# Two-layer mixer and expert kernel: earlier picks for the context tokens, attention heads in pairs, and the latents' query products and key scores split by tile

## The chip, the cores and the metric

One core of one Trainium2 chip runs one launch. The metric is the device time of that launch in microseconds (us); lower is better. The figure for a kernel is the median of its runs.

## What is computed

The reference is one step of a network with two layers over 128 context tokens and 512 latent tokens, 1024 features each, all in 32-bit floats. Per layer and per group of tokens:

```python
h = rmsnorm(x, P['norm_mix_g']) * (1.0 + sc_m) + sh_m
proj = h @ P['w_in']
# attention (8 query heads, 2 key/value heads, 64 wide), hyena (long convolution by FFT), chunked gating
mixed = jnp.concatenate([attn, hy, sg], axis=-1) @ P['w_out']
x = x + g_m * mixed
h = rmsnorm(x, P['norm_ffn_g']) * (1.0 + sc_f) + sh_f
x = x + g_f * peer(h, P['peer_wq'], P['peer_keys'], P['peer_u'], P['peer_v'])
```

and in `peer`, for each token and each of 8 heads:

```python
q = (x @ wq).reshape(T, PEER_HEADS, 2, PEER_HALF)
s = jnp.einsum('thpd,hpnd->thpn', q, keys)          # 2 x 128 scores
s_top, i_top = lax.top_k(s, 16)                     # 16 of each 128
cand = s_top[..., 0, :, None] + s_top[..., 1, None, :]
sc, pos = lax.top_k(cand, 16)                       # 16 of 256
gate = softmax(sc)
a = gelu(einsum('td,ted->te', xt, u_tab[idx]))      # 16 rows of 1024 per token and head
out = einsum('te,ted->td', gate * a, v_tab[idx])    # 16 more
```

The latents' attention has 128 cached and 512 own keys; the context's has its own 128. The convolution's filter is made from a small network of sines (jobs f1, f2, f3) and a transform (job hf), and does not depend on the tokens.

## The kernel before, in words

**Tiles and groups.** The 640 tokens are five tiles of 128: four of latents (index L_ = 0) and one of context (C_ = 1). The work is two kinds of job. A mixer job is one product with what follows it (qk, vt, hy, su, df, cv, attention, wo, the second norm, wq, ka and kb). An expert step is one unit, which is one head of one tile: 16 experts for each of 128 tokens. There are four groups of units, `GROUPS` = context of layer 0 (8 units), latents of layer 0 (32), context of layer 1 (8), latents of layer 1 (32), 80 units in all.

**One expert step** (`step_jobs`, L175). Step u has 16 pieces. Each has a `dot` of unit u on VectorE (L1415: the gathered row times the token's features, summed) and an `add` of unit u-1. For context units the add is one VectorE operation (L1429); for latent units it is two products on TensorE by a diagonal (L885), whose diagonal ScalarE makes from an identity (L1113). Between the pieces VectorE picks the experts of unit u+1: `stage` (ScalarE copies 256 scores, L1094), then six parts of `pick` (L1373 and on) with 27 linked steps: the 16 best of each 128 scores, the 16 best of the 256 sums, and the index by one-hot rows (L1395 to L1398, twice over 256 elements). Last in a step come `weigh` and `gexp`.

**The gathers.** GpSimd issues 32 indirect transfers per unit (`fetch`, L610), one u row and one v row in turn, each 128 rows of 4 KB. Rows land in a ring of 4 places per table, so a transfer is issued when a dot or an add has freed its place, and GpSimd waits in order.

**The weights.** SyncE streams blocks of 1 MB through a ring of 4 slots (`STREAM`, L298). A block is issued when the last product of the block four places ahead is done. The 0.5 MB of expert keys is the last block of each mixer. Before layer 1's blocks, `small_loads` waits for the latents' last kb.

**The order.** `ORDER` (L225) is one list that every engine walks in order, taking its part of each job. `weave` puts expert jobs between mixer jobs in proportion to the costs in `ROOM`. In sequence:

- the context's mixer of layer 0 alone, then the pick of unit 0 (`start_jobs`);
- the latents' mixer of layer 0, woven with the 9 steps of the first context group (units 0 to 7 of the trace);
- the context's mixer of layer 1, woven with steps 0 to 16 of the first latent group (units 8 to 24);
- steps 17 to 32 of that group alone (units 25 to 39 and the last adds), then the pick of unit 40;
- the latents' mixer of layer 1, woven with the second context group (units 40 to 47);
- the second latent group alone (units 48 to 79), and the output.

In the latents' mixers all of wq (8 jobs of 8 products, 512 columns, L700) comes first, then ka and kb (L865: scores of 4 heads, ka from rows 0 to 63, kb from rows 64 to 127). The first latent unit is picked after the scores of tile 0, and its first dot waits for `ht` (L872), the transpose of the tile's features.

**Attention of the latents.** 32 units, one head and one tile each: scores over 640 keys with 64 rows of the array (L813, L814), the maximum on VectorE (L1334), the exponential on ScalarE (L1075), a reciprocal and a diagonal on VectorE (L1339, L1343), five transposes that also scale (L823), a copy on ScalarE (L1082), and five products with the values that fill 64 of the output's rows (L835). Scores of unit n+3 wait for the copy of unit n.

**TensorE in 32-bit.** Every product shows as two records in the trace.

## Time and profile before

| | us |
|---|---|
| median of 3 runs | 4240.7 |
| lowest and highest | 4236.87, 4241.16 |
| the profiled execution | 4239.37 |
| its span, first to last instruction | 4237.5 |

The profiled execution lies 1.3 us below the median, and the span leaves 1.9 us of it outside. Busy time is the time in which an engine runs an instruction. In windows, each engine has its busy time and, in brackets, its number of instructions; PEclk is the share of 2.4 GHz that TensorE's clock was granted, and the last number is what the DMA engines moved in GB/s. In lines of the timeline, the number in square brackets is how long the engine stood idle before, and what ended that.

### The profile page before, as it was taken

The numbers are of one execution on the slowest core, as the hardware profiler recorded it, in microseconds if no ns is written. First come the engines' busy times: TensorE is split into PE (matmuls) and PEld (weight loads), VectorE is DVE, ScalarE is ACT, GpSimd is POOL, SyncE is SP. The second block draws the span as 40 slices with busy tenths as digits, with TensorE's granted clock in tenths as the row PEclk, the third lists the DMA queues.
The fourth block names the chain that finished last, engine by engine and source line by source line (L and its number), as shares of the span: only waits on it lengthen the run. The fifth ranks groups of instructions, "written<-read, shape, count | busy, mean of one in ns | idle before, by whom it ended". The sixth has DMA issues, their size and how long they took to land.

```text
span 4237.5 us, 33926 instructions
## 1 busy us (share of the span) xinstructions
PE 3274.7 (77%) x9680; PEld 1513.7 (36%) x9680; DVE 2951.7 (70%) x6826; ACT 1065.3 (25%) x2256; POOL 2563.5 (60%) x2564
## 2 busy tenths in 40 slices
PE   6797896577778787777776978975777777777777
PEld 4653653233333333222222536542222222222223
DVE  2388998545667666677764889897676767677673
ACT  4322322122222222222223323221222222222222
POOL 0054666345656666777773545566777777777774
PEclk8898998689999999999998988987999999999999
DMA  7587788899989999999995877788999999999998
GB/s 281 215 314 276 262 297 287 330 378 369 381 332 384 379 407 386 408 409 401 409 407 191 318 277 244 275 303 336 409 407 395 407 409 400 409 406 401 401 409 313
DMA packets 394007, 1485.64 MB, mean 351 GB/s; under 512 B 44124, under 2 KB 46878, under 8 KB 377952
## 3 DMA queue, kind: packets, MB, share of 16 engines
q0 software_dynamic: 368640, 1342.34, 82.5%
q1 hardware_dynamic: 25184, 141.13, 8.6%
q8 instruction: 81, 1.33, 0.1%
q14 instruction: 102, 0.84, 0.1%
HBM read 1480.42 MB, written 2.88 MB: 350 GB/s over the span
## 4 chain that ended last, share of the span: by engine, by line
DMA 25%; DVE 21%; PE 19%; POOL 18%; issue 13%; ACT 4%; SPq 0%; DVEq 0%; ACTq 0%; POOLq 0%
POOL rows_ring L610 18%; DMA rows_ring<-in_peer_u,idx 13%; DMA rows_ring<-in_peer_v,idx 11%; PE psum L885 8%; DVE rows_ring L1415 7%; DVE mix L1429 4%; PE psum L700 4%; PE psum L687 1%; PE psum L823 1%; DVE small L1334 1%; PE psum L656 1%; DMA ring<-in_ada 1%; DVE pos L1362 1%; DVE pos L1359 1%; DVE cand L1360 1%
## 5 line engine op out<-in xcount | busy, mean ns | idle before, releaser
L885 PE MATMUL psum<-rows_ring,diag 128*128 128x512 f32 x4096 | 2042.7, 627 | 674.9 <-DMA rows_ring<-in_peer_v,idx 544.5
L610 POOL DMA_INDIRECT rows_ring<-in_peer_u,idx x1280 | 1298.0, 1014 | 1015.5 <-DVE rows_ring L1415 475.3
L1415 DVE SCALAR_TENSOR_TENSOR rows_ring<-rows_ring,psum 128x1024 f32<-128x1024 f32 x1024 | 1240.7, 1220 | 678.9 <-DMA rows_ring<-in_peer_u,idx 639.7
L610 POOL DMA_INDIRECT rows_ring<-in_peer_v,idx x1280 | 1265.2, 988 | 634.2 <-issue 306.6
L885 PEld LDWEIGHTS psum<-rows_ring,diag 128*128 128x128 f32 x4096 | 717.3, 193 | 1937.6 <-DMA rows_ring<-in_peer_v,idx 1231.7
L1113 ACT ACTIVATE diag<-ident,wts 128x128 f32<-128x128 f32 x1024 | 382.3, 397 | 1333.3 <-PE psum L885 1332.6
L700 PE MATMUL psum<-area,ring 128*128 128x128 f32 (+1 forms) x1344 | 386.7, 447 | 15.6 <-ACT area L975 14.9
L1429 DVE SCALAR_TENSOR_TENSOR mix<-rows_ring,wts,mix 128x1024 f32<-128x1024 f32 x254 | 326.4, 1285 | 15.5 <-DMA rows_ring<-in_peer_v,idx 13.9
L1415 DVE SCALAR_TENSOR_TENSOR rows_ring<-rows_ring,area 128x1024 f32<-128x1024 f32 x256 | 311.9, 1222 | 13.5 <-DMA rows_ring<-in_peer_u,idx 12.0
L700 PEld LDWEIGHTS psum<-area,ring 128*128 128x128 f32 x1344 | 216.3, 200 | 195.0 <-issue 191.7
L700 PE MATMUL psum<-mix,ring 128*128 128x128 f32 (+1 forms) x512 | 143.0, 441 | 2.9 <-DVE mix L1354 2.1
L1105 ACT ACTIVATE acts<-dots 128x16 f32<-128x16 f32 x80 | 17.3, 216 | 498.4 <-DVE rows_ring L1415 498.3
L823 PE MATMUL psum<-sg_junk,area 128*128 128x128 f32 x672 | 109.5, 314 | 37.0 <-DVE sg_junk L1343 37.0
L823 PEld LDWEIGHTS psum<-sg_junk,area 128*128 128x128 f32 x672 | 93.5, 214 | 53.8 <-DVE sg_junk L1343 43.5
L1101 ACT ACT_TABLE_LOAD x75 | 96.2, 1283 | 41.0 <-DVE wts L1440 41.0
L700 PEld LDWEIGHTS psum<-mix,ring 128*128 128x128 f32 x512 | 80.8, 198 | 67.3 <-issue 63.6
L835 PE MATMUL psum<-area,v_tok 128*64 128x128 f32 x672 | 102.4, 304 | 0.0
L1075 ACT ACTIVATE area<-psum,small 128x640 f32<-128x640 f32 (+1 forms) x80 | 56.9, 711 | 176.0 <-DVE small L1334 175.9
L1105 ACT ACT_TABLE_LOAD x78 | 100.1, 1283 | 1.4
L813 PE MATMUL psum<-area 64*128 64x512 f32 x128 | 81.6, 720 | 13.3 <-ACT area L1082 6.7
L1082 ACT COPY area<-psum 128x640 f32<-128x640 f32 (+1 forms) x80 | 48.5, 606 | 161.3 <-PE psum L823 161.3
L835 PEld LDWEIGHTS psum<-area,v_tok 128*64 128x64 f32 x672 | 81.4, 152 | 15.7 <-issue 9.3
(176 smaller groups left out, 2497.3 us busy)
## 6 DMA issues: line engine op xcount, KB each, us to landing
ring<-in_ada SPq DMA_DIRECT2D x48, 1024.0 KB, 8.2
ring<-in_win SPq DMA_DIRECT2D x32, 1024.0 KB, 8.1
rows_ring<-in_peer_u,idx POOLq DMA_INDIRECT x1280, 7.2
rows_ring<-in_peer_v,idx POOLq DMA_INDIRECT x1280, 7.1
ring<-in_wout SPq DMA_DIRECT2D x16, 1024.0 KB, 8.0
ring<-in_wq SPq DMA_DIRECT2D x16, 1024.0 KB, 7.8
ring<-in_dft SPq DMA_DIRECT2D x12, 1024.0 KB, 7.8
xT<-in_xT_in SPq DMA_DIRECT2D x1, 2048.0 KB, 13.1
```

Source lines behind the costliest of these rows:

```text
L610: pool.indirect_dma_start(row(table, k), None, (peer_u, peer_v)[table], bass.IndirectOffsetOnAxis(ap=idx[u % IDX_PLACES][:, k:k + 1], axis ...
L700: m = pe.matmul(g[:, 0:WIDTH[st]], w[:, k * P:(k + 1) * P], src(k), start=(k == 0), stop=(k == KC - 1))
L813: pe.matmul(g[:, 0:512], q, kT[st][rows, 0:512], start=True, stop=True)
L823: m = pe.matmul(att_bank(st, n)[:, b * P:(b + 1) * P], probs[st][:, n % 2, b * P:(b + 1) * P], softmax_diag[:, n % 2, :], start=True, stop ...
L835: m = pe.matmul(out_bank(st, c)[rows, t * P:(t + 1) * P], v_tok[:, b, rows], probsT[st][:, n % 2, i * P:(i + 1) * P], start=(i == 0), stop ...
L885: m = pe.matmul(acc[:, b, :], diag[:, k % 4, :], row(1, k)[:, b * 512:(b + 1) * 512], start=(u % PEER_HEADS == 0 and k == 0), stop=last)
L1075: act.activation(probs[st][:, n % 2, :], att_bank(st, n)[:, 0:KEYS[st]], ACT.Exp, bias=negmax[:, n % 2:n % 2 + 1], accum_out=rowsum[:, n % ...
L1101: act.activation(gate_e[:], best[:], ACT.Exp, bias=gate_s[:, 1:2], accum_out=gate_s[:, 0:1]).then_inc(s["gexp_ready"], 1)
L1105: act.activation(acts[:], dots[:], ACT.Gelu_apprx_tanh).then_inc(s["gelu_ready"], 1)
L1113: act.activation(diag[:, k % 4, :], ident[:], ACT.Copy, scale=wts[:, k:k + 1]).then_inc(s["diag_ready"], 1)
L1415: dve.scalar_tensor_tensor(out=row(0, k), in0=row(0, k), scalar=1.0, in1=h, op0=ALU.mult, op1=ALU.mult, accum_out=dots[:, k:k + 1]).then_i ...
L1429: m = dve.scalar_tensor_tensor(out=out_tok[C_], in0=x, scalar=wts[:, k:k + 1], in1=out_tok[C_], op0=ALU.mult, op1=ALU.add)
```

## The change

- **Picks.** The scores are read where they lie, without the copy on ScalarE. The pick has 8 parts with 24 links, and the two one-hot halves are one operation over 512 elements. The 8 units of the second context group are picked in steps 21 to 28 of the first latent group, each behind that step's own pick, into index and gate places of their own (`idx_c`, `gate_c`). No `start_jobs` stands ahead of that group.
- **Filter.** Layer 1's filter jobs (f1, f2, f3, hf; 2 MB of transform blocks) move from the latents' mixer to steps 26 to 32 of the first latent group.
- **Attention.** The latents' heads go in pairs. Two heads' scores alternate between rows 0 to 63 and 64 to 127 of the array and end in different PSUM banks, and their value products alternate between output rows 0 to 63 and 64 to 127. The softmax diagonal moves from VectorE to ScalarE. The next scores wait for the copy of the pair two ahead of them.
- **Query products and scores.** wq of the latents covers the first tile's 128 columns, followed by that tile's scores and the pick. The other 384 columns (8 jobs wr) and the 12 other score jobs are woven with steps 0 to 3 of the latent group. The latents' keys go to the place of `sq` and not through the ring. ka and kb are issued alternately, head by head. The context's layer 1 mixer is woven with steps 4 to 20 instead of 0 to 16.

```diff
+    if st == L_:
+        n = ATT_UNITS[L_] // 2
+        jobs = [("fence", l, st, 0), ("pas", l, st, 0), ("pas", l, st, 1)]
+        for m in range(n):
+            jobs += [("pat", l, st, m)] + ([("pav", l, st, m - 1)] if m else [])
+            jobs += [("pas", l, st, m + 2)] if m + 2 < n else []
...
...
+def filter_jobs(l):
...
...
-        jobs += js("f3:0 f3:1 f3:2 f3:3 hf:0 hf:1 hf:2 hf:3")
+        jobs = js("rms:0 app:0") if l else js("f3:0 f3:1 f3:2 f3:3 hf:0 hf:1 hf:2 hf:3")
         jobs += js("qk:0 vt:0 hs:0 vt:1 vt:2 rot:0 vt:3 hy:0 ck:0 hy:1 hy:2 hy:3 hy:4 hy:5 su:0 ut:0 su:1 ut:1 "
                   "qk:1 sp:0 hs:1 qk:2 rot:1 hs:2 qk:3 rot:2 hs:3 qk:4 rot:3 hs:4 sp:1 df:0 rot:4 df:1 df:2 df:3 cv:0 cv:1")
...
+        if st == L_ and i == 1:
+            return jobs
...
+def late_jobs(l):
...
+    jobs = [("wr", l, L_, j) for j in range(KC)]
+    for i in range(2, 2 * LAT_TILES):
+        jobs += [("ka", l, L_, i), ("kb", l, L_, i)]
+    return jobs
...
+PICK_AT = (0, 1, 3, 4, 6, 7, 9, 10)
...
+PICKED_AHEAD = (2,)
+AHEAD_FROM = 21
...
+    own = u + 1 < n and grp not in PICKED_AHEAD
...
-        jobs += [("pick", grp, u + 1, p // 2)] if u + 1 < n and p % 2 and p // 2 < PICK_PARTS else []
+        if own and ahead and p < PICK_PARTS:
+            jobs += pick_jobs(grp, u + 1, [p])
+        elif own and not ahead and p in PICK_AT:
+            jobs += pick_jobs(grp, u + 1, [PICK_AT.index(p)])
+        if ahead and p >= PICK_PARTS:
+            jobs += pick_jobs(*ahead, [p - PICK_PARTS])
...
+    jobs += [("gexp", grp, u + 1, 0)] if own else []
+    jobs += [("gexp", *ahead, 0)] if ahead else []
...
+        v = u - AHEAD_FROM
+        early = grp + 1 in PICKED_AHEAD and 0 <= v < UNITS[grp + 1]
+        out += step_jobs(grp, u, (grp + 1, v) if early else None)
...
-    _a = 0
+    _a = LATE_STEPS
+    ORDER += weave(late_jobs(_l), expert_jobs(_g, range(_a)))
     if _l + 1 < DEPTH:
-        _a = PEER_HEADS * 2 + 1
-        ORDER += weave(mixer_jobs(_l + 1, C_), expert_jobs(_g, range(_a)))
-    ORDER += expert_jobs(_g, range(_a, UNITS[_g] + 1))
-    if _l + 1 < DEPTH:
-        ORDER += start_jobs(_g + 1)
...
+        ORDER += weave(mixer_jobs(_l + 1, C_), expert_jobs(_g, range(LATE_STEPS, _a)))
+        ORDER += expert_jobs(_g, range(_a, FILTER_FROM))
+        _a = FILTER_FROM
+        ORDER += weave(filter_jobs(_l + 1), expert_jobs(_g, range(_a, UNITS[_g] + 1)))
+    else:
+        ORDER += expert_jobs(_g, range(_a, UNITS[_g] + 1))
...
+                if (kind, st, i) == ("wq", L_, 3):
...
+                    sp.dma_start(sq_cols[:, :], keysT[l].rearrange("p a b -> p (a b)")).then_inc(s["keys_loaded"], 16)
...
+            def pair_scores(l, st, m):
...
+                for n, a, b in ((2 * m, 512, 640), (2 * m + 1, 128, 640), (2 * m, 0, 512), (2 * m + 1, 0, 128)):
+                    c, rows, t = unit_of(st, n)
+                    if (a, b) == (0, 128):
+                        pe.wait_ge(s["pair_first"], done("pas", l, st, m))
+                    ins = pe.matmul(att_bank(st, n)[:, a:b], qT[st][rows, c, t * P:(t + 1) * P], kT[st][rows, a:b], start=True, stop=True)
...
+                blocks = [TILES, 0, 1, 2, 3]
+                for i, b in enumerate(blocks):
+                    for n in (2 * m, 2 * m + 1):
+                        _, rows, _ = unit_of(st, n)
+                        ins = pe.matmul(out_bank(st, c)[rows, t * P:(t + 1) * P], v_tok[:, b, rows], probsT[st][:, n % 2, i * P:(i + 1) * P],
+                                        start=(i == 0), stop=(i == len(blocks) - 1))
+                ins.then_inc(s["pair_out"], 1)
...
+                project(st, half_of(blk("wq", l, st, j // 2), j % 2), g, lambda k: hT[st][:, k, 0:P], "h_ready",
+                        KC * NUMBER["app", l, st, 1], width=P).then_inc(s["wq_mm"], 1)
+            def wr(l, st, j, g):
+                project(st, half_of(blk("wq", l, st, j // 2), j % 2), g, lambda k: hT[st][:, k, P:LAT], width=LAT - P
+                        ).then_inc(s["wr_mm"], 1)
...
+                    for half, rows in ((0, slice(0, 64)), (1, slice(64, P))):
+                        m = pe.matmul(out[half][:, h * P:(h + 1) * P], mix[rows, h0 + h, a:a + P], keys[rows, h0 + h, :],
+                                      start=True, stop=True)
+                        if h == 3:
+                            m.then_inc(s[("ka_mm", "kb_mm")[half]], 1)
...
+            def pair_diag(l, st, m):
+                for n in (2 * m, 2 * m + 1):
+                    act.wait_ge(s["pair_rinv"], 2 * NUMBER["pat", l, st, m] + n % 2 + 1)
+                    act.activation(softmax_diag[:, n % 2, :], ident[:], ACT.Copy, scale=rinv[:, n % 2:n % 2 + 1]
+                                   ).then_inc(s["pair_diag"], 1)
...
                 step(dve.max(vals[:, 8:16], src))
                 step(dve.max_index(idxs[:, 8:16], vals[:, 8:16], src))
-            def pick(grp, u, to, part):
...
+                if part < 4:
+                    half = part // 2
+                    vals, idxs = topv[:, half, :], topi[:, half, :]
+                    src = scores[st][:, (2 * u + half) * N_KEYS:(2 * u + half + 1) * N_KEYS]
+                    if part % 2 == 0:
+                        top8(vals, idxs, src, step)
+                        step(dve.match_replace(src, vals[:, 0:8], src, -3.0e38))
...
+                    step(dve.tensor_tensor(pair, iota16.unsqueeze(1).unsqueeze(1).broadcast_to(two),
+                                           posf.unsqueeze(3).broadcast_to(two), ALU.is_equal))
...
-                    half, oh = part - 4, grid(onehot[:, :], TOPK)
-                    step(dve.tensor_tensor(oh, iota16.unsqueeze(1).broadcast_to(square),
-                                           posf[:, half, :].unsqueeze(2).broadcast_to(square), ALU.is_equal))
-                    step(dve.tensor_tensor(oh, oh, topf[:, half, :].unsqueeze(1).broadcast_to(square), ALU.mult))
-                    step(dve.tensor_reduce(picked[:, half, :], oh, AX.X, ALU.add))
...
+                    step(dve.tensor_tensor(pair, pair, topf.unsqueeze(2).broadcast_to(two), ALU.mult))
+                    step(dve.tensor_reduce(picked, pair, AX.X, ALU.add))
...
+                    dve.tensor_scalar(idx_of(grp, u), idxf[:], float(l * N_EXPERTS), None, ALU.add).then_inc(s["idx_ready"], 1)
```

## Rows read from the trace of the kernel before

**Rows 1.** The page: GB/s in 40 slices of the span.

```profile
GB/s 281 215 314 276 262 297 287 330 378 369 381 332 384 379 407 386 408 409 401 409 407 191 318 277 244 275 303 336 409 407 395 407 409 400 409 406 401 401 409 313
```

**Rows 2.** Windows by stage: length, busy us (x instructions), PEclk, DMA share, GB/s.

```profile
211.70:774.40 562.70, 460.16 (x1761) 276.96 (x1765) 484.73 (x918) 145.35 (x248) 318.82 (x257) 0.88 0.80 285
774.40:1627.80 853.40, 644.39 (x1980) 298.14 (x1979) 527.94 (x1362) 206.13 (x500) 502.03 (x532) 0.92 0.97 376
1627.80:2247.30 619.50, 476.40 (x980) 165.59 (x980) 431.71 (x1058) 141.44 (x327) 450.00 (x475) 1.00 1.02 404
...
2284.20:2870.50 586.30, 479.75 (x1769) 286.27 (x1769) 511.46 (x986) 167.83 (x279) 309.25 (x260) 0.86 0.74 266
```

**Rows 3.** Windows inside the second layer's latent mixer.

```profile
2304.00:2358.00 54.00, 32.49 (x91) 19.98 (x92) 44.62 (x101) 14.95 (x21) 17.65 (x15) 0.68 0.43 139
2358.00:2531.00 173.00, 150.74 (x478) 82.56 (x476) 153.50 (x286) 52.12 (x81) 90.31 (x77) 0.94 0.82 303
2531.00:2698.00 167.00, 143.29 (x768) 108.45 (x768) 152.08 (x312) 57.44 (x109) 93.00 (x76) 0.85 0.73 249
2698.00:2754.00 56.00, 55.51 (x130) 24.66 (x131) 47.95 (x88) 3.25 (x7) 32.39 (x29) 1.00 0.85 318
...
2769.00:2827.00 58.00, 57.25 (x128) 25.03 (x128) 54.92 (x71) 14.24 (x22) 41.20 (x37) 0.96 0.92 347
```

**Rows 4.** Windows inside the first layer's latent mixer.

```profile
648.00:714.00 66.00, 57.89 (x129) 25.18 (x129) 51.73 (x67) 13.86 (x22) 46.17 (x35) 0.91 0.84 287
714.00:774.40 60.40, 27.64 (x164) 22.02 (x168) 37.77 (x73) 7.36 (x14) 23.31 (x17) 0.57 0.71 244
```

**Rows 5.** Timeline, second layer's start: start, us, operation, idle before.

```profile
2284.16 0.28 DVE L1358 MAX8 topv<-unit_s 128x8 f32<-128x128 f32 x1
...
2294.67 0.17 DVE L1402 TENSOR_SCALAR idx<-idxf 128x16 uint32<-128x16 f32 x1
...
2308.82 1.22 DVE L1415 SCALAR_TENSOR_TENSOR rows_ring<-rows_ring,area 128x1024 f32<-128x1024 f32 x1
```

**Rows 6.** Timeline, VectorE: the first dot of the first latent group.

```profile
774.45 1.22 DVE L1415 SCALAR_TENSOR_TENSOR rows_ring<-rows_ring,psum 128x1024 f32<-128x1024 f32 x1 [13.69 <-PE psum L872]
```

**Rows 7.** Lines of VectorE, 2308 to 2871: busy us, mean ns, idle.

```profile
L1343 DVE TENSOR_SCALAR sg_junk<-ident,small 128x128 f32<-128x128 f32 x32 | 9.9, 311 | 1.1
L1397 DVE TENSOR_TENSOR onehot<-onehot,topf 128x256 f32<-128x256 f32 x16 | 6.8, 425 | 0.5
...
L1326 DVE COPY area<-psum 128x512 f32<-128x512 f32 x8 | 5.5, 684 | 0.9 <-PE psum L865 0.9
...
L1202 DVE SCALAR_TENSOR_TENSOR area<-area 64x512 f32<-64x512 f32 x6 | 4.1, 683 | 0.2
```

**Rows 8.** Lines of TensorE, the same stretch.

```profile
L687 PE MATMUL psum<-area,ring 128*128 128x256 f32 x128 | 32.7, 421 | 5.3 <-issue 5.3
L865 PE MATMUL psum<-ring,mix 64*128 64x128 f32 x128 | 18.9, 370 | 16.1 <-DVE area L1326 8.8 <-ACT area L1068 6.5 <-ACT mix L1064 0.7
```

**Rows 9.** Timeline, TensorE: the query products of the second layer.

```profile
2769.07 57.25 PE L700 MATMUL psum<-area,ring 128*128 128x512 f32 x128 [7.32 <-ACT area L975]
```

**Rows 10.** Timeline, TensorE: adds of latent experts alone.

```profile
2247.32 8.85 PE L885 MATMUL psum<-rows_ring,diag 128*128 128x512 f32 x20 [0.54 <-DMA rows_ring<-in_peer_v,idx]
```

**Rows 11.** Timeline, TensorE: two column halves taken in turn.

```profile
326.31 1.09 PE L767 MATMUL psum<-sgwT,sg_v 128*64 128x128 f32 x16
```

**Rows 12.** Timeline, TensorE: one attention unit.

```profile
487.19 1.31 PE L835 MATMUL psum<-area,v_tok 128*64 128x128 f32 x10
488.43 1.12 PE L813 MATMUL psum<-area 64*128 64x512 f32 x2
489.39 0.38 PE L814 MATMUL psum<-area 64*128 64x128 f32 x2
```

**Rows 13.** The page: a diagonal made on ScalarE, and the landing of a row.

```profile
L1113 ACT ACTIVATE diag<-ident,wts 128x128 f32<-128x128 f32 x1024 | 382.3, 397 | 1333.3 <-PE psum L885 1332.6
...
rows_ring<-in_peer_v,idx POOLq DMA_INDIRECT x1280, 7.1
```

More of the change, by code:

```diff
@@ L111, in phase @@
     return 2 * l + (st == L_)
+FILTER_FROM = 26
+LATE_STEPS = 4
+def filter_jobs(l):
+    return [("f1", l, L_, 0), ("f2", l, L_, 0)] + [(k, l, L_, t) for k in ("f3", "hf") for t in range(LAT_TILES)]
 def mixer_jobs(l, st):
@@ L241 @@
     _count[_job[0]] = NUMBER[_job] + 1
+    if _job[0] == "pick":
+        PICK.setdefault(_job[1:3], len(PICK))
+LAST_GEXP, _last = {}, {}
+for _job in ORDER:
+    if _job[0] == "pick" and _job[3] == 4:
+        LAST_GEXP[_job[1:3]] = _last.get(GROUPS[_job[1]][1])
+    elif _job[0] == "gexp":
+        _last[GROUPS[_job[1]][1]] = _job
 def done(*job):
```

296 lines of the change are left out of this document (191 added, 105 removed).

## The prediction

> **What bounds the kernel now.** I read the page's 40 slices first (106 us each), then windows by stage. The page shows long stretches at 400 to 410 GB/s, and two valleys: below 331 up to slice 8, and at 191 to 336 in slices 22 to 28 [rows 1]. No row anywhere exceeds about 410, so where the gathers run at that rate, only fewer bytes or a removed stop help. The stage windows give the boundaries [rows 2]:
>
> - 211.7 to 774.4, layer 0's latent mixer with 8 context units: 562.7 us at 285 GB/s, VectorE busy 484.7, TensorE 460.2.
> - 774.4 to 1627.8, 17 latent units with a context mixer: 853.4 us at 376 GB/s.
> - 1627.8 to 2247.3, 15 latent units alone: 619.5 us at 404 GB/s, so 41.3 us a unit. VectorE is busy 431.7, or 28.8 us a unit.
> - 2284.2 to 2870.5, layer 1's latent mixer: 586.3 us at 266 GB/s, VectorE 511.5, TensorE 479.8.
>
> Inside the mixers the bound moves [rows 3]. Attention (2531 to 2698) has VectorE busy 152.1 of 167. Projections and convolution (2358 to 2531) have both engines at 150 to 154 of 173. The stage of w_out and that of the query products are TensorE's: 55.5 of 56 and 57.3 of 58. So work taken from VectorE shortens the two mixers, and the split query products shorten a stage that TensorE holds.
>
> **The change, part by part.** The sum is against the profiled 4239.4 us, 1.3 below the median.
>
> *The pick.* One pick alone runs from 2284.16 to 2294.84, 10.7 us [rows 5]. Six operations over 256 elements at 0.43 become three over 512, for which the nearest row is a copy at 0.68 [rows 7]: 0.5 us less, so 10.2. No row shows a 512-wide one-hot; at twice 0.43 it saves nothing, and I take 0.5. Beside the latents' experts it lies in slack; in the first mixer 8 picks give 4 us.
>
> *Layer 1's latent mixer.* Off VectorE go the pick of unit 40 (10.7) and 7 more (about 10 of busy time each, 70), 32 diagonals of 0.31 (9.9), 6 of 8 key copies at 0.68 (4.1), and the filter: two chains of three operations at 0.68 and four shorter ones (estimated at 4.2 each), and four times one of 0.68 and two of 0.43 (6.2), 14.5 in all [rows 5, 7]. That is 109, leaving 402 of 511. Of VectorE's 75 us of idle time, the 9 around the filter chain, 6 of the 8 under w_out and 2 of the 3 beside wq go [rows 3], and I add 6 where picks filled gaps, as ahead of the first norm: its chain still ran 14.0 us past the pick's end [rows 5]. So 402 + 64 = 466: a gain of 120. Against it stand in-order waits and the DMA: w_out to wq have 884 of the mixer's 2528 `ROOM` points, so 35% of the 134 MB of rows (256 transfers of 0.52), plus 8 MB of weights, 55 MB or 135 us at 409 GB/s, where VectorE alone would allow about 130. I take 105, and keep 120 as one end and 75 as the other (all removed work but a third given back as waits).
>
> *Layer 0's latent mixer.* Its picks and filter stay. Off VectorE go 9.9, 4.1 and 4. The wq stage has VectorE idle for 14.3 of 66 us with TensorE at 57.9, and the last stage ends in 13.7 us of idle VectorE before the first dot [rows 4, 6], where the transposes stand in TensorE's queue behind products whose weights were requested only after the last kb. Of the 14.3 I count 11 as gone, with TensorE's share cut to a quarter, and of the 13.7 all, as unit 8 starts behind tile 0's scores; w_out, as above, gives 6. The total is 18 + 11 + 14 + 6 = 49, of which I take 40; ends 20 and 50. The wait for those weights does not vanish: it falls into step 4 of the latent group, where TensorE's adds queue behind it. I charge 5 there.
>
> *Attention pairs.* An existing line shows column pairs: 16 records with the halves alternating take 1.09 us, 10 one-sided ones of the same size 1.31 [rows 11, 12], so the value products about halve, 20 us of TensorE a layer. No row shows two row groups at once; between serial and halved, scores of 1.34 us a unit [rows 12] save 0 to 21. As VectorE holds the stage, I credit neither on the path. ScalarE gains 32 diagonals at 0.40 [rows 13], 13 us on an engine busy 57.4 of 167 [rows 3]: hidden, but each diagonal is now one more hop between engines; with dots and adds between the hops I price that at nothing; if they run dry, 0.3 us on each of 32 units is 10 a layer. The Trainium skill (TensorEngine Tiling, Overview) gives up to 2x for a contraction of 64 rows, which no row here shows for row groups. Read as the gain of the stage, that page gives the rival of paired products below, 4069 us. The same page (PSUM Bottleneck) says that tiling does not speed up the emptying of PSUM, and by that, as by VectorE's 152.1 of 167 us there [rows 3], the time stays as summed.
>
> *The late jobs, twice.* Eight wr jobs are 3/4 of the 57.3 us of wq [rows 9], 43 us, and the key jobs 3/4 of 18.9 [rows 8], 14. TensorE is busy 31.8 of 41.3 us in a unit alone [rows 2], so four steps have 38 spare, and 57 do not quite fit. The nearest row is the context mixer's stage: 104 us of TensorE above the adds' share, 42 MB of weights (103 us), 853.4 us against 17 x 41.3 + 103 = 805. So 48 lost for 104 us of mixer. That price gives 26; the low end is 0, since much of TensorE's busy time is its waiting tail. I take 15 per layer, 30 in all. ScalarE's and VectorE's copies (0.4 to 0.7 each) hide in slack.
>
> *Steps 21 to 32.* Two picks raise VectorE from 28.8 to about 39 of 41.3 us: nearly full, so 6 over eight steps. Filter work of 14.5 falls mostly on steps 26 to 28, with 7 spare: 7. The transform has half of the 32.7 us of its line [rows 8], four jobs of 4 us on TensorE, with the short ones 26 us: 7 for its stops. The 2 MB of blocks cost 5 at 409 GB/s, in the stage that is DMA-bound. Sum 25, ends 10 and 50.
>
> *The start.* About 1, for a lighter pick and no staged copy.
>
> Sum: -1 - 40 + 15 + 5 + 25 - 105 + 15 = -86, so 4153 us.
>
> **The rivals.**
>
> *Freed time turns into waiting.* VectorE's work is gone, but TensorE's order, its clock and the hops hold the mixers. For it: projections have TensorE at 150.7 of 173 [rows 3], and the granted clock is 0.85 in attention [rows 3] and 0.57 in layer 0's key stage [rows 4], where TensorE is least busy; fewer products may leave it more often at the lower of its two levels. Against: TensorE also loses about 120 us in layer 1 (43 + 14 + 26 + 20 and the scores' part). The mixers would give 20 and 60 instead of 40 and 105: 4218.
>
> *Slower: long TensorE jobs empty the gather rings.* Place: the 16 wr jobs in the first four steps of each latent group. Each is 5.4 us between adds, GpSimd stops on the next v row, and a new row takes 7.1 us to land [rows 13]. If each job costs its length and half a landing, 8.9, the 16 cost 143 instead of the 30 that all late jobs have in the sum: 4153 + 113 = 4266. It decides against the change from about 8 us a job. Against: 8 rows in flight are 10 us of DMA, and an add's pair of products takes 1.8 us where it doesn't wait (20 records, four to an add, in 8.85 [rows 10]) while the DMA brings a u and a v row in 2.6 (41.3/16), so TensorE catches up; weights of similar length ran beside experts at 376 GB/s.
>
> *VectorE overflows in steps 21 to 28.* If two picks and the dots no longer hide in the DMA's pace and a step takes 46 us, eight steps cost 38 where 6 stand: 4185.
>
> *Everything fits.* Late jobs and filter cost 15 together, and the mixers give 120 and 49: 4239 - 1 - 169 + 15 + 5 = about 4090.
>
> *Paired products on the path.* If TensorE held attention, halved scores and value products (32 x 1.34 and 32 x 1.31 us a layer [rows 12], 42 of 85) would come on top: 4153 - 84 = 4069. Against it: VectorE's load there.
>
> *The change does little*, because attention stays serial or the picks wait for something: covered by the first.
>
> **How the numbers follow.** Chances: forecast 0.53, freed time waiting 0.17, slower 0.08, overflow 0.08, all fits 0.11, pairs on the path 0.03. The forecast's own range by its bounds is 4110 to 4205. The range to hold 8 in 10 takes most of the good and the first bad rival: 4090 to 4222. A change of 0.2%, 8.5 us, is what a measurement of this kernel can tell from none: faster 0.88, the same 0.04, slower 0.08.
>
> **What would show it.** Right: the first dot of unit 8 near 734, that of unit 40 at most 20 us after the last latent add, unit 48 some 465 to 490 us after the end of group two's last adds; steps 21 to 28 at 42 to 44 us; no pick lines between units 40 and 47; steps 0 to 3 of each latent group at 43 to 48 us, with GpSimd's waits on TensorE grown there. Wrong: idle VectorE of over 100 us in either mixer, steps of over 50 us, or GB/s under 350 in a latent group's first four steps.

## The result, and the profile after

The changed kernel takes 4276.0 us (median of 4 runs, 4274.3 to 4282.3) against 4238.8 of the kernel before, run beside it: a ratio of 1.0093, 95% interval 1.0076 to 1.0111. It is slower by 0.9%; the forecast was 4153, and its range ended at 4222.

The profiled execution took 4274.3 us, with a span of 4272.5. The page's GB/s in 40 slices, after:

```profile
GB/s 283 228 323 272 266 317 261 310 328 366 389 350 387 376 377 372 390 384 382 334 368 364 262 322 308 335 230 315 344 409 398 409 408 400 409 405 402 406 409 311
```

The valley of layer 1's mixer is shallower (262, 322, 308, 335 in slices 23 to 26, where there were 318, 277, 244, 275 [rows 1]). But the level ahead of it has gone: slices 17 to 21, five times 401 or more before, now stand at 390 to 334. And slices 8 and 9, the first steps of the latent group, fell from 330 and 378 to 310 and 328.

Windows by stage, after (length, busy us and instructions of each engine, granted clock, DMA share, GB/s):

```profile
207.00:742.30 535.30, 367.79 (x1677) 235.03 (x1677) 471.76 (x859) 144.01 (x269) 306.60 (x257) 0.84 0.80 287
742.30:934.90 192.60, 130.73 (x381) 61.48 (x382) 118.00 (x283) 31.87 (x78) 106.82 (x114) 0.88 0.85 310
934.90:1029.50 94.60, 57.80 (x198) 23.64 (x197) 31.18 (x84) 18.06 (x45) 32.78 (x35) 0.82 0.95 373
1773.90:2377.20 603.30, 458.59 (x1009) 179.41 (x1009) 430.83 (x1130) 141.64 (x319) 377.01 (x397) 0.95 0.93 355
2377.20:2875.40 498.20, 347.87 (x1610) 218.44 (x1608) 404.94 (x607) 132.02 (x246) 302.70 (x256) 0.86 0.82 302
2875.40:3063.70 188.30, 129.49 (x381) 60.93 (x382) 117.73 (x282) 31.88 (x77) 106.73 (x114) 0.88 0.87 316
```

They are, in order: layer 0's latent mixer (first dot of unit 0 to first dot of unit 8), the four late steps, step 4, the units 28 to 40, layer 1's latent mixer (units 40 to 48), and its four late steps. Set against the same stretches of before, from first dot to first dot, the whole difference of 35.0 us between the spans (4237.5 and 4272.5) is:

| stretch | before | after | difference | forecast |
|---|---|---|---|---|
| to unit 0 | 211.7 | 207.0 | -4.7 | -1 |
| units 0 to 8, layer 0's latent mixer | 562.7 | 535.3 | -27.4 | -40 |
| units 8 to 28, late jobs and context mixer | 978.8 | 1031.6 | +52.8 | +20 |
| units 28 to 40, two picks a step, filter | 555.6 | 603.3 | +47.6 | +25 |
| units 40 to 48, layer 1's latent mixer | 561.7 | 498.2 | -63.5 | -105 |
| units 48 to 52, late jobs | 156.3 | 188.3 | +32.0 | +15 |
| the rest | 1210.7 | 1208.8 | -1.9 | 0 |

So the mixers did become shorter. VectorE is busy 404.9 us in the second, 92 less than before (496.9), where the forecast counted 109 less from 2284.2 on, 98 of it in this stretch (the rest is the pick of unit 40 ahead of it). The groups of steps outside the mixers cost more than charged.

The forecast drew its border between steps and mixer at the last latent add (2280.1 before, 2355.6 after), the table at the first dot of unit 40. By the forecast's border, steps 21 to 32 grew by 49.2 us (486.0 to 535.2) where 25 stood, and layer 1's latent mixer gave 70.6 (590.4 to 519.8) where 105 stood. Of the table's 47.6, 5.5 us is unit 28, where the displaced context mixer now ends (40.9 to 46.4).

**One wr job in layer 1**, from the timeline of the changed kernel (start, us, operation, idle time before and its releaser):

```profile
2930.43 1.45 PE L1017 MATMUL psum<-rows_ring,diag 128*128 128x512 f32 x3
2931.72 5.32 PE L792 MATMUL psum<-area,ring 128*128 128x384 f32 x16
2938.00 7.53 PE L1017 MATMUL psum<-rows_ring,diag 128*128 128x512 f32 x17 [0.96 <-ACT diag L1262]
...
2937.08 0.48 ACT L1201 COPY mix<-psum 128x384 f32<-128x384 f32 x1 [13.47 <-PE psum L792]
2937.46 1.28 ACT L1262 ACTIVATE diag<-ident,wts 128x128 f32<-128x128 f32 x4
...
2935.58 0.93 POOL L702 DMA_INDIRECT rows_ring<-in_peer_u,idx  x1 [0.30 <-DVE rows_ring L1597]
2940.23 0.94 POOL L702 DMA_INDIRECT rows_ring<-in_peer_v,idx  x1 [3.72 <-PE psum L1017]
```

TensorE runs 5.32 us of products between adds. ScalarE has stood idle for 13.47 us until they ended, because the copy of wr's bank is ahead of the next diagonals in its order, so after the job TensorE waits another 0.96 us for a diagonal. GpSimd's next row of v needs a place that only an add frees: 3.72 us without a gather. Over the whole span the page puts 382.2 us of GpSimd's idle time ahead of the latents' rows of v down to TensorE's adds; on the page of before the largest part was issue, 306.6.

In step 4 TensorE waits for the modulation's weights, as was forecast, but for longer:

```profile
932.80 3.67 PE L1017 MATMUL psum<-rows_ring,diag 128*128 128x512 f32 x8 [1.06 <-ACT diag L1262]
951.65 1.93 PE L748 MATMUL psum<-ring,cwide 128*32 128x512 f32 x8 [15.18 <-DMA ring<-in_ada]
```

Inside layer 1's latent mixer, after, the windows that answer to [rows 3], from attention on:

```profile
2564.00:2690.00 126.00, 87.48 (x748) 74.91 (x748) 113.38 (x179) 60.02 (x132) 80.52 (x70) 0.91 0.87 307
2690.00:2749.00 59.00, 56.51 (x148) 25.32 (x148) 45.33 (x60) 2.79 (x4) 39.64 (x35) 1.00 0.88 339
2749.00:2779.00 30.00, 9.87 (x16) 3.47 (x16) 15.57 (x22) 9.26 (x14) 16.09 (x13) 0.72 0.85 338
2779.00:2799.00 20.00, 18.89 (x128) 17.31 (x128) 19.24 (x28) 8.29 (x15) 12.07 (x10) 0.83 0.54 177
2799.00:2825.00 26.00, 0.00 (x0) 0.00 (x0) 22.90 (x28) 0.39 (x3) 20.24 (x18) 0.53 0.99 375
2825.00:2875.40 50.40, 19.93 (x80) 13.30 (x80) 34.32 (x65) 4.67 (x9) 20.91 (x18) 0.60 0.51 167
```

The query products fell from 58 to 20 us, and then TensorE does nothing at all for 26 us, while VectorE works through experts and the gathers run at 375 GB/s. The weave gives the one-tile product the weight of the four-tile one (55), so experts that had their place beside 58 us of products now stand ahead of the keys.

### The profile page after: what moved, and what is told of

Same layout as the page of the kernel before. It is cut to its first block, busy times and chain, and to the rows that moved or that the text cites. A ratio compares the mean times of both kernels' runs of the same rounds, so it can differ in the third digit from the quotient of the medians.

```text
span 4272.5 us, 34224 instructions
## 1 busy us (share of the span) xinstructions
PE 3156.5 (74%) x9936; PEld 1486.1 (35%) x9936; DVE 2893.5 (68%) x6522; ACT 1034.8 (24%) x2247; POOL 2549.4 (60%) x2564
## 4 chain that ended last, share of the span: by engine, by line
DMA 27%; PE 24%; POOL 17%; DVE 15%; issue 12%; ACT 5%; SPq 0%; DVEq 0%; ACTq 0%; POOLq 0%
DMA rows_ring<-in_peer_v,idx 18%; POOL rows_ring L702 17%; PE psum L1017 13%; DMA rows_ring<-in_peer_u,idx 6%; DVE rows_ring L1597 5%; PE psum L792 4%; DVE mix L1611 3%; DMA rows_ring<-in_peer_v,idx_c 2%; PE psum L779 1%; DVE small L1512 1%; PE psum L748 1%; PE psum L741 1%; ACT area L1226 1%; ACT diag L1262 1%; DMA ring<-in_ada 1%
## 5 line engine op out<-in xcount | busy, mean ns | idle before, releaser
L1017 PEld LDWEIGHTS psum<-rows_ring,diag 128*128 128x128 f32 x4096 | 735.5, 196 | 1944.8 <-DMA rows_ring<-in_peer_v,idx 1058.3
L702 POOL DMA_INDIRECT rows_ring<-in_peer_v,idx x1024 | 965.2, 943 | 591.7 <-PE psum L1017 382.2
L702 POOL DMA_INDIRECT rows_ring<-in_peer_u,idx x1024 | 973.7, 951 | 498.6 <-issue 269.7
L702 POOL DMA_INDIRECT rows_ring<-in_peer_u,idx_c x256 | 318.0, 1242 | 442.1 <-DVE idx_c L1584 202.0
L792 PE MATMUL psum<-area,ring 128*128 128x128 f32 (+2 forms) x1600 | 402.6, 410 | 21.0 <-ACT area L1108 17.5
L702 POOL DMA_INDIRECT rows_ring<-in_peer_v,idx_c x256 | 292.3, 1142 | 167.3 <-DVE mix L1611 103.5
L792 PEld LDWEIGHTS psum<-area,ring 128*128 128x128 f32 x1600 | 253.5, 204 | 182.7 <-issue 149.1
L1254 ACT ACTIVATE acts<-dots 128x16 f32<-128x16 f32 x80 | 17.3, 216 | 576.4 <-DVE rows_ring L1597 576.1
L1226 ACT ACTIVATE area<-psum,small 128x640 f32<-128x640 f32 x64 | 50.2, 789 | 206.4 <-DVE small L1512 206.4
L913 PE MATMUL psum<-area 64*128 64x128 f32 (+1 forms) x256 | 46.5, 488 | 61.4 <-ACT area L1234 55.5
L1597 DVE DVE_READ_ACCUMULATOR rows_ring<-rows_ring,psum 128x1 f32 x1024 | 84.4, 82 | 0.0
```

The costliest lines, as they stand in the source:

```text
L702: pool.indirect_dma_start(row(table, k), None, (peer_u, peer_v)[table], bass.IndirectOffsetOnAxis(ap=idx_of(grp, u)[:, k:k + 1], axis=0)). ...
L792: m = pe.matmul(g[:, 0:width or WIDTH[st]], w[:, k * P:(k + 1) * P], src(k), start=(k == 0), stop=(k == KC - 1))
L913: ins = pe.matmul(att_bank(st, n)[:, a:b], qT[st][rows, c, t * P:(t + 1) * P], kT[st][rows, a:b], start=True, stop=True)
L1017: m = pe.matmul(acc[:, b, :], diag[:, k % 4, :], row(1, k)[:, b * 512:(b + 1) * 512], start=(u % PEER_HEADS == 0 and k == 0), stop=last)
L1226: act.activation(probs[st][m % 2][:, n % 2, :], att_bank(st, n), ACT.Exp, bias=negmax[:, n % 2:n % 2 + 1], accum_out=rowsum[:, n % 2:n % 2 ...
L1254: act.activation(acts[:], dots[:], ACT.Gelu_apprx_tanh).then_inc(s["gelu_ready"], 1)
```

## The experiments

Four questions: what the late jobs cost and by which mechanism, what the filter jobs cost, what each moved or paired part gives the mixers, and whether a version beats the kernel before. "Ratio" is against the kernel before, run beside each, where the changed kernel has 1.0093. How far one profile carries differs by stretch. Runs 6, 9, 10 and 11 have the same code up to unit 12, and their units 0 to 8 take 531.6 to 547.6 us; so a difference of up to 16 us in layer 0's latent mixer shows nothing (runs 2 and 7, which differ from them only behind it, have 547.2 and 559.4). Layer 1's latent mixer has the same code in runs 6, 9 and 10, and takes 478.2 to 481.2 us there. Units are counted over the whole kernel, from first dot to first dot; where an expectation says steps 12 to 15, 33 to 35 or 49 and 50, it means the units of these numbers (unit 8 is step 0 of layer 0's latent group, unit 48 that of layer 1's).

**1. The weave's weight of the one-tile query product.**

```diff
+    room = lambda j: 14 if (j[0], j[2]) == ("wq", L_) else ROOM[j[0]]
...
-        cost += ROOM[job[0]]
+        cost += room(job)
```

> The changed kernel with one number altered: the cost that the weave gives a latent wq job is 14 instead of 55, since the job now has a quarter of its products. Theory (the split gained little because a fifth of the context experts is still placed beside wq, so that TensorE stands idle between wq and the keys for some 26 to 35 us): the experts move ahead, the first key job comes sooner after wq, and each latent mixer shortens by 5 to 15 us: 4276 becomes 4250 to 4265. Rival (the tail of each latent mixer is set by the last context unit's own dots, adds and transfers, whatever stands beside them): no change, 4270 to 4280, and the key jobs move but unit 8 and unit 48 start when they did.

4257.7 us, ratio 1.0051 [1.0032, 1.0071]. Units 40 to 48 took 481.4 us instead of 498.2; layer 0's mixer shows no gain (541.8 against 535.4, within its spread). So 17 us of the missing gain was a number in a table.

**2. The late jobs back in the latent mixers.** With edit 1; and no expert job between the two halves ka and kb of a key job.

```diff
+    if st == L_:
+        jobs += [("wr", l, st, j) for j in range(KC)]
...
-    _a = LATE_STEPS
-    ORDER += weave(late_jobs(_l), expert_jobs(_g, range(_a)))
+    _a = 0
...
-        _a = AHEAD_FROM
-        ORDER += weave(mixer_jobs(_l + 1, C_), expert_jobs(_g, range(LATE_STEPS, _a)))
+        _a = PEER_HEADS * 2 + 1
+        ORDER += weave(mixer_jobs(_l + 1, C_), expert_jobs(_g, range(_a)))
```

> The changed kernel with the late jobs (wr and six of eight key score pairs) put back into the latent mixers, ahead of and behind the first tile's scores as before, the two halves of the query products together costed as before, and the context mixer woven with steps 0 to 16 again. Theory (late jobs cost the latent stages 28 and 32 us where I had 15 each, and push the stream of modulation weights into a stage that is bound by DMA, 20 to 35 us more): the first four latent units return to 41 to 43 us outside the modulation phase, the stop of some 20 us at the start of the modulation jobs goes, and the mixers grow by 10 to 30 each; total 4215 to 4250. Rival (the loss is not in the late jobs but in the picks ahead and the filter): 4270 to 4310.

4177.3 us, ratio 0.9866 [0.9845, 0.9886]: a larger gain than the expected 4215 to 4250, and faster than before. Units 48 to 52 take 156.9 us as before (156.3), and the mixer that has the jobs back takes 483.1 against 481.4 without them. Moving them out of it gained 2 us there.

**3. The context not picked ahead.**

```diff
-PICKED_AHEAD = (2,)
+PICKED_AHEAD = ()
...
+        ORDER += start_jobs(_g + 1)
```

> The changed kernel without the early picks of the second context group: its picks come in its own steps, and the first one stands behind the last latent unit, as before. Theory (the early picks cost about 10 us in steps 21 to 28 and give 40 to 70 us in the layer 1 latent mixer): slower, 4310 to 4330, with steps 21 to 25 back near 41 us. Rival (two picks in a step delay the dots by more than they save): 4276 or faster.

4298.3 us, ratio 1.0144 [1.0123, 1.0165], between the two expectations: picking ahead is worth 22 us. Units 40 to 48 are 38.3 us longer without it, unit 39 to 40 8 longer; and the units 28 to 39 are 21 us shorter, so two picks in a step cost more than the 6 us charged for eight steps. VectorE is busy 466.7 us in the units 40 to 48 here and 404.9 in the changed kernel: the seven picks are 61.8 us there, 8.8 each, where the forecast had 10 each.

**4. Layer 1's filter jobs back in its latent mixer.**

```diff
-        jobs = js("rms:0 app:0") if l else js("f3:0 f3:1 f3:2 f3:3 hf:0 hf:1 hf:2 hf:3")
+        jobs = js("rms:0 app:0 f1:0 f2:0") if l else []
+        jobs += js("f3:0 f3:1 f3:2 f3:3 hf:0 hf:1 hf:2 hf:3")
...
-        ORDER += weave(filter_jobs(_l + 1), expert_jobs(_g, range(_a, UNITS[_g] + 1)))
+        ORDER += expert_jobs(_g, range(FILTER_FROM, UNITS[_g] + 1))
```

> The changed kernel with layer 1's filter jobs back in its latent mixer. Theory (in steps 26 to 32 they cost 25 to 35 us, since the chain f1, f2, f3 and four transform jobs hold queues that each carry the experts, and in the mixer they cost about the same, as it now has idle VectorE time): 4265 to 4285, with steps 25 to 31 back at 41 to 43 us and the mixer longer by 25 to 35. Rival (they fill gaps in the mixer): 4245 to 4260. Rival (they were well hidden in the latent steps): 4295 to 4310.

4248.9 us, ratio 1.0028 [1.0009, 1.0048], as the first rival said (the runs spread from 4233 to 4259, and the profiled one is the fastest). Units 33 to 39 fall from 282.7 to 257.6 us, 39 to 40 from 100.0 to 93.8, and the mixer rises only from 498.2 to 504.0.

**5. ScalarE copies later.** The bank of wr, and of layer 1's hf, is copied two adds later in ScalarE's own order.

```diff
+                if kind == "wr" or (kind == "hf" and a):
+                    behind.append([job, 2])
+                elif kind in jobs:
...
+                for late in behind if kind == "add" or (kind == "dot" and b == 0) else []:
+                    late[1] -= 1
+                while behind and behind[0][1] <= 0:
+                    (kind, a, b, n), _ = behind.pop(0)
+                    jobs[kind](a, b, n, psum[:, BANK[kind, a, b, n], :])
```

> The changed kernel, only that ScalarE copies each bank of wr, and of layer 1's spectra hf, two adds (or two first-step dots) later in its own order: the four diagonal matrices ahead of TensorE are then made before ScalarE stands still for the long TensorE job. In steps 1 to 3 of layer 1 the changed kernel shows ScalarE waiting 78.2 us for wr's TensorE job in 6 waits (up to 15.8 us), and behind them TensorE and the gather queue stand. Theory (the stall is ScalarE's, which holds the diagonals back): the four late steps of each layer lose 15 to 25 us of their 28 and 32 us over plain steps, steps 33 to 35 lose 8 to 15 us, and the time falls by 35 to 60 us against the changed kernel (4216 to 4241). Rival (the length of the TensorE job, 5.3 us of matmuls, is what the rings can't bridge, and the diagonal adds only its 0.96 us each time): 5 to 15 us less (4261 to 4271), and steps 49 and 50 stay above 49 us.

4242.6 us, ratio 1.0029 [1.0015, 1.0044]. By the ratios that is 27 us below the changed kernel, between the two expectations (35 to 60, and 5 to 15). The late steps lost 10.5 us in layer 1 (188.3 to 177.8) and 15.7 in layer 0 (192.6 to 176.9), a third to a half of their cost; units 33 to 35 lost nothing (51.9, 55.2, 46.8 us). TensorE's waits over the units 49 and 50 of this kernel:

```profile
PE psum L1017 <- ACT diag L1262: 36.5, 1, 36.5
PE psum L1017 <- DMA rows_ring<-in_peer_v,idx: 9.0, 9, 2.4
```

The one wait for a diagonal is that at the group's start, before any add; the others are gone in these two units (5.3 us of them remain in unit 51). Yet the four steps still take 21 us more than plain ones, which leaves the length of the TensorE job itself.

**6. Late jobs back, context mixer still from step 4 on.**

```diff
-    _a = LATE_STEPS
-    ORDER += weave(late_jobs(_l), expert_jobs(_g, range(_a)))
+    _a = LATE_STEPS if _l + 1 < DEPTH else 0
+    ORDER += expert_jobs(_g, range(_a))
```

> The run with the late jobs back in the latent mixer, only that the context mixer is again woven with steps 4 to 20, as in the changed kernel, with steps 0 to 3 plain. It parts the two things that the late jobs did: their own steps, and the displacement of the context mixer into 17 steps that begin at step 4. Theory (late jobs cost by themselves and by displacement): steps 0 to 3 at 41 to 42 us, the modulation's steps 12 to 15 at 55 to 62 each as in the changed kernel, and a total 10 to 25 us above the 4177 us of the run with the mixer from step 0 (4187 to 4202). Rival (displacement costs nothing, the modulation takes its time anywhere): within 6 us of 4177. Rival (the displacement is most of the cost): 4215 or more.

4171.3 us, ratio 0.9867 [0.9841, 0.9894], as run 2, and as the first rival said: the displacement of the context mixer costs nothing in the total. Units 8 to 12 take 164.6 us, and unit 12 takes 72.2 instead of 94.6, without the 15 us wait:

```profile
742.20:906.80 164.60, 96.78 (x191) 33.74 (x192) 113.94 (x276) 28.44 (x65) 108.45 (x115) 0.87 0.99 387
906.80:979.00 72.20, 50.70 (x196) 21.02 (x195) 31.16 (x84) 17.07 (x45) 31.83 (x34) 0.92 1.02 413
```

With the changed kernel's 192.6 and 94.6 this prices the late jobs: 28.0 + 22.4 = 50.4 us in layer 0, and in layer 1 188.3 - 157.2 = 31.1. In the runs 1, 3 and 4, which have the same late jobs, the prices come out at 42 to 45 and 29 to 34.

**7. Late jobs and filter back (mixer from step 0).** Edits 2 and 4.

> Late jobs back and filter jobs of layer 1 back in its latent mixer: what is left of the change is the fine picks, the context picked ahead and the paired attention. If the two costs add: 4177 less 27 is 4150 us (4143 to 4158). If they overlap (the filter jobs in the mixer now meet the other jobs that were put back, so that VectorE or TensorE there becomes the bound): 4160 to 4180.

4166.8 us, ratio 0.9849 [0.9825, 0.9873]: the two costs overlap, as the second expectation had it (the profiled execution, 4183.5 us, is the slowest of the four). Units 28 to 40 lose 34.6 us, the mixer gets 24 of them (507.1 against 483.1).

**8. All wr jobs in step 0.** The changed kernel with edit 1, and:

```diff
-    ORDER += weave(late_jobs(_l), expert_jobs(_g, range(_a)))
+    ORDER += weave(late_jobs(_l)[:KC], expert_jobs(_g, range(1)))
+    ORDER += weave(late_jobs(_l)[KC:], expert_jobs(_g, range(1, _a)))
```

> The changed kernel with the first run's edit (the one-tile query product counts 14 in the weave) and all 8 wr jobs in step 0, where no adds run and TensorE was busy 0.00 of 32.0 us; the 12 late key jobs stand in steps 1 to 3. Same jobs, same ranges of steps. Theory (a long TensorE job costs where it stands between adds, because it holds ScalarE's diagonals and the gather queue behind it; between dots alone it is free): step 0 at 32 to 40 us, steps 1 to 3 at 42 to 44 each, so the four steps fall from 192.6 and 188.3 us to 158 to 172; step 12's wait for the modulation's weights shortens too, since wr gives its ring slots back earlier: 72 to 85 us instead of 94.6. Time 4257.7 less 45 to 75: 4183 to 4213. Rival (the late jobs cost by their sum on TensorE, wherever they stand): 4245 to 4258.

4177.2 us, ratio 0.9878 [0.9859, 0.9898]: 80 us less than run 1 for the same jobs in the same four steps. The first two windows are layer 0's four steps and its step 4, the third layer 1's four steps:

```profile
744.10:915.40 171.30, 134.40 (x379) 57.92 (x377) 117.56 (x283) 35.69 (x80) 109.07 (x116) 0.95 0.98 378
915.40:988.20 72.80, 53.39 (x195) 22.28 (x195) 30.92 (x84) 16.13 (x42) 31.24 (x33) 0.88 1.01 407
...
2804.20:2960.70 156.50, 128.68 (x375) 55.99 (x374) 117.49 (x282) 34.68 (x78) 107.06 (x115) 0.98 0.98 379
```

TensorE is as busy as in the changed kernel (128.7 against 129.5 us in layer 1), but the DMA share is 0.98 instead of 0.87, and the steps are as long as without late jobs (157.2 in run 6). Nor is it the granted clock: the same work keeps TensorE busy 129.5 us at 0.88 and 128.7 at 0.98. In step 0 there are no adds: with wr there TensorE is busy 29.39 of 32 us and nothing is lost:

```profile
2804.20:2836.20 32.00, 29.39 (x104) 17.34 (x102) 28.22 (x70) 4.52 (x9) 16.19 (x18) 0.99 0.81 269
```

ScalarE's waits for key jobs, 34.5 us in the steps 1 to 3, remain in this run and cost nothing. So the sum on TensorE is not the cost, and a waiting ScalarE alone isn't either; it is a TensorE job of 5 us between adds, with the diagonals held behind it (run 5) as a part. Two of a layer's eight wr jobs run before the latent group's first dot in both kernels, and six stand between adds in run 1. Moving these saves 34.7 us in layer 1 (191.2 to 156.5), about 6 us a job. In layer 0 it saves 37.3 over steps 0 to 4 (281.4 to 244.1), but 20.8 of that is unit 12, where the wait for the modulation's weights goes, and 16.6 the four steps. They keep 6.6 us over run 6 (171.2 against 164.6): unit 11 takes 55.1 us with a DMA share of 1.03 at 400 GB/s, where weights now pass.

The traces also show the link from the TensorE job to the time. This is how long GpSimd waited for a place, over the four late steps of layer 1, in the order of the steps' length:

| kernel | four steps | GpSimd waits for TensorE | for VectorE | both |
|---|---|---|---|---|
| run 1 | 191.2 | 35.8 | 24.4 | 60.2 |
| changed kernel | 188.3 | 34.0 | 24.0 | 58.0 |
| run 5, copies later | 177.8 | 29.7 | 18.2 | 47.9 |
| run 6, no late jobs | 157.2 | 7.2 | 17.3 | 24.5 |
| run 8, wr in step 0 | 156.5 | 5.6 | 16.4 | 22.0 |

The waits of the changed kernel and of the runs 1 and 5 exceed those of run 6 by 33.5, 35.7 and 23.4 us, and their steps are longer by 31.1, 34.0 and 20.6.

**9 and 10. The filter from step 29; and the filter's sines and copies two adds later on ScalarE.** Both on run 6.

```diff
-FILTER_FROM = 26
+FILTER_FROM = 29
```

> The run with late jobs back and the context mixer from step 4, only that layer 1's filter jobs begin with step 29 instead of 26, behind the last of the eight steps with two picks. There VectorE is busy 28.8 us of 41 in a step, in steps 26 to 28 it is 37.5 of 41.6 before any filter job. Theory (the filter jobs cost because VectorE is full in these steps): the units 33 to 40 take 382.8 us in the base and lose 12 to 20 here, time 4151 to 4159. Rival (the cost is ScalarE's wait for the sine's argument and TensorE's jobs, with the diagonals held behind, wherever they stand): the loss only moves to steps 29 to 31, time 4166 to 4176.

4171.0 us, ratio 0.9849 [0.9833, 0.9865], as the rival said. Units 33 to 40 take 375.2 instead of 382.8 us. Units 33 to 35 are back at 47.3, 41.9 and 42.3, but units 36 to 38 now take 48.6, 49.7 and 45.6.

```diff
+                if kind in ("f1", "f2", "hf") and a:
+                    behind.append([job, 2])
```

> The same base (4171 us), filter jobs from step 26, but ScalarE takes the two sines and the copies of the spectra two adds later in its own order, so that it makes the diagonals first (it stood 13.2 us for the second sine's argument in the changed kernel, between 2051.7 and 2064.9). Theory (VectorE is full): no more than 5 us saved, 4164 to 4172. Rival (the held diagonals): steps 33 to 35 lose 10 to 15 us of their 22 over plain ones, 4155 to 4162.

4172.6 us, ratio 0.9855 [0.9839, 0.9872], not the rival's gain: units 33 to 40 take 376.0 us, units 33 to 35 keep 51.8, 50.5 and 46.3. Each of the two causes, VectorE's fullness and the held diagonals, is worth 7 us in the stretch, and the time can't tell either from nothing. Without filter jobs the stretch takes 349.5 us (run 11), so 26 us of their cost remain after either edit. No run has both edits, and which hop of the filter's chain costs the rest stays open.

**11. Late jobs and filter back, context mixer from step 4.** Edits 4 and 6.

> The same base with the filter jobs back in layer 1's latent mixer. The run with both back and the mixer from step 0 was 4166.8, 10.6 below its own base where 27 was expected. If that pair's gain is 27 as between the changed kernel and its filter run: 4144; if it is 10 again: 4161.

4158.9 us, ratio 0.9833 [0.9816, 0.9849]: the fastest run. Units 28 to 40 fall by 31.5 us (598.8 to 567.3), the mixer takes back 20.9 (481.2 to 502.1).

**12. wr in step 0, filter back.** Edits 4 and 8.

> The run with all wr jobs in step 0 (4177.2), and layer 1's filter jobs back in its latent mixer: the whole of the change but the moved filter, with the wr jobs where no adds run. With everything late put back, the filter's return saved 12.4 us (4171.3 to 4158.9). If it is the same here: 4161 to 4169. If the filter jobs find more room in this mixer, from which wr and the late keys are gone (theory: there TensorE sets the time beside VectorE): 4148 to 4158.

4181.4 us, ratio 0.9872 [0.985, 0.9895], outside both expectations: no gain over run 8. Units 28 to 40 lose 30.6 us, and units 40 to 48 grow by 30.3 (478.7 to 509.0). The mixer without wr and late keys has no more room for the filter than the one with them.

**13. The attention unpaired.** Run 8 with the attention of before: one head and tile at a time, the diagonal on VectorE.

```diff
-    if st == L_:
+    if False:
         n = ATT_UNITS[L_] // 2
...
-            c, t, half = n // 2 // NT[st], n // 2 % NT[st], n % 2
+            c, half, t = n // (2 * NT[st]), n // NT[st] % 2, n % NT[st]
...
-            return psum_cols[:, a:a + PAST + LAT]
+            return psum_cols[:, 1024 * (1 + n % 3):1024 * (2 + n % 3)]
```

> The run with all wr jobs in step 0 (4177.2), only that the latents' attention takes one unit (head and tile) at a time again, with the diagonal of the softmax made on VectorE, as in the kernel before. Theory (the pairs shorten the attention's stage, which stood at 167 us before and 126 after in layer 1): 25 to 45 us more in each of the two latent mixers, 4227 to 4260. Rival (the experts woven into the mixer set its time, by VectorE at 403 of 479 us and the gathers, so that the attention's time is only moved): within 15 us in each, 4180 to 4205.

4195.0 us, ratio 0.9907 [0.989, 0.9923], as the rival said. Windows of layer 1's attention, here from its first exponential to its last, and in run 8 from the load of the exponential's table, 5.3 us ahead of the first one, to the last:

```profile
2535.10:2678.10 143.00, 119.80 (x708) 90.78 (x709) 136.37 (x230) 56.74 (x103) 106.20 (x87) 0.95 0.91 322
```

```profile
2535.40:2659.90 124.50, 86.21 (x703) 73.38 (x700) 111.81 (x177) 58.99 (x128) 79.06 (x72) 0.86 0.88 313
```

From first exponential to last it is 119.4 us in run 8 (2540.7 to 2660.1, TensorE busy 83.8), so the stage is 23.6 us shorter with pairs, and TensorE's busy time 36.0 less; units 40 to 48 keep 16.1 of it (494.7 against 478.7). In layer 0 the exponentials span 127.4 us instead of 154.8, and units 0 to 8 take 536.3 and 536.4: nothing of it is seen there, in a stretch whose spread is 16 us. The edit also puts the diagonals back on VectorE (9.9 us a layer before [rows 7]), so how much of the 16 us is the pairing itself isn't parted.

## Why the prediction was wrong, step by step

**The late jobs** are the largest step that failed: 15 us a layer and 5 for the wait in step 4 were charged, 35 in all, and the runs show 50 in layer 0 (42 to 45 by the runs 1, 3 and 4) and 31 in layer 1. The forecast took as nearest row the price of a mixer beside experts, per us of TensorE. But the cost is not per us: the same TensorE work is free in step 0 and costs about 6 us a job between adds (layer 1, run 8). That was the mechanism of the rival "long TensorE jobs empty the gather rings", which got 0.08. Its price was 8.9 us for each of 16 jobs, 143 in all; measured are about 6 for each of the six that stand between adds in layer 1, and 81 for all late jobs of both layers. So it is in part luck that its 4266 lies near the measured 4276: other terms made up the rest. The argument against it was that TensorE catches up between jobs. It does, but the gathers can't: in plain steps the DMA share is 1.02 [rows 2], so the 3.72 us in which GpSimd issues nothing are not regained (the table of run 8: waits and steps grow together). The slack that counts is that of the resource that is full. Part of the price, a third in layer 1, is ScalarE's order, which the rival didn't name. The wait in step 4 was seen, and sized at 5 where unit 12 grows by 22.4; it is gone where wr gives back its slots of the weights' ring earlier (runs 6 and 8).

**Steps 21 to 32** were charged 25 and cost 47.6 up to unit 40's first dot, 49.2 by the forecast's own border. The filter is 31 to 36 of that (runs 4, 7, 11 and 12). The context's picks are most of the rest: 6 stood for eight steps, and with the filter away (run 11) the units 29 to 36 take 344.7 us against 331.0 before, so 14; beside the filter they cost up to 21 (run 3). In layer 1's mixer the same filter jobs take 6 to 30 us: 24.0, 20.9 and 30.3 in the three kernels with the mended weight. The sum gave their move a gain in the mixer and a small price outside; it is a trade that at best comes out even; in run 11, undoing it wins 10.6 us in the two stretches (14 by the ratios).

**Layer 1's latent mixer** was to give 105 and gave 63.5 (70.6 by the forecast's border). VectorE's busy time fell nearly as counted (by 92 of 98), but its idle time rose from 65 us (561.7 - 496.9) to 93. From the last latent add on it rose from 77 to 108, where the sum had 64 and, with the 105 it took, 79. Of the 41 missing, 17 are the weave's weight of wq (run 1). By parts: picking ahead 38, with 61.8 us of VectorE's work removed from the stretch (run 3), so six tenths; pairs with the diagonals' move 16; the late jobs 2 (run 2 against run 1). With the weight mended the stretch gave 80 to 83, inside the forecast's ends. "Freed time turns into waiting", the first rival, had the mixers' gain at 20 and 60; with 27.4 and 63.5 measured, its numbers fit the mixers, and the slower rival's mechanism the late steps. Of the causes that the first rival named, the order is shown, for 17 us (run 1); the clock and the hops were not parted.

**Layer 0's latent mixer** was to give 40: the first dot of unit 8 came at 742.3, with 734 forecast and 774.4 before [rows 6]. Of this term 32 of 40 came, 4.7 of it from the start; a window of 35 us without any TensorE work (659 to 694) stands there too. With the stretch's spread of 16 us, the 12.6 us that are missing are not shown to be more than chance.

**The pairs** were credited with nothing on the path, and gave up to 16 us in layer 1 (with the diagonals' move) and nothing that shows in layer 0. The column pairs' row was right: a pair's 20 value records take the time of 10 before [rows 12], and so do the scores. These are one pair's lines in the changed kernel:

```profile
2590.38 1.35 PE L913 MATMUL psum<-area 64*128 64x128 f32 x8 [1.44 <-ACT area L1234]
2591.66 2.50 PE L922 MATMUL psum<-sg_junk,area 128*128 128x128 f32 x20
2594.09 1.31 PE L935 MATMUL psum<-area,v_tok 128*64 128x128 f32 x20
```

**What pointed wrong in the signs named:** steps of over 50 us (52.3 and 58.1 in layer 1) and GB/s under 350 in a latent group's first steps (310 and 316). Both were named ahead as what would refute the sum. VectorE's idle time in layer 1's mixer, the third, is 93.3 us from unit 40's first dot and 107.9 from the last latent add, where over 100 was named.

The part of the change that pays is the pick ahead, the pairs and the lighter VectorE; what the finer parts of the pick give by themselves no run shows. With late jobs and filter back (run 11) it is 1.7% faster than the kernel before: at its ratio, 4239 x 0.9833 = 4168.

## What to carry to other kernels

Before a job moves to a stretch that looks idle on its engine, ask what that engine frees for others, and how full the receiving stretch is: between adds that give gathers their places, a TensorE job of 5 us cost about 6 us of a DMA-bound step, and in the one step without adds eight of them were free. Where jobs are woven by a table of weights, a job that shrinks needs its weight shrunk too. And work moved out of a stage with several almost full resources gives back only a part: 92 us less for VectorE (496.9 to 404.9) brought 63 here.

## What the runs showed of the hardware

Two products over 64 rows each, in different halves of the array's rows, run at the same time: the four score products of a pair (512 and 128 columns for each of two heads) take 1.35 us, where those of one head took 1.34, from the first's start to the second's end, before [rows 12]. The forecast left this open between serial and halved. It is the doubling that the Trainium skill (TensorEngine Tiling, Overview) states as the upper bound for a dimension of 64; the trace agrees. The transposes between them, over 128 rows and columns, gained little: 2.50 us for two units, where one unit's took 1.38 before.

The granted clock of TensorE was 0.53 in the 26 us in which it had no work, so nearly all of them at the lower of its two levels (1.2 of 2.4 GHz), and 0.60 in the key stage behind them; in run 8's first step, where wr fills TensorE, it is 0.99, and in the changed kernel's four late steps 0.88.
